# Half of the next block's scores between transposes and values' products in cross attention, and a local gate part behind the fourth transposes

## The chip, the cores and the metric

The kernel runs on one core of one Trainium2 chip. The metric is the device time in microseconds from launch to end of the whole program. A core has TensorE (matmuls and transposes, with weight loads that overlap them), VectorE, ScalarE, GpSimd, and SyncE, which here issues the DMAs. Each engine runs its own list of instructions in order; engines wait for each other on semaphores.

## The reference

One step of a one-layer hybrid decoder for two groups of requests: a prompt of 1024 tokens and 8 samples of 4 tokens each, 1056 tokens in all, with width 1024. All is in 32-bit floats.

```
xn = rmsnorm(x, norm_mix_g)
aq, ak, av, dq, dk, dvv, dz, da, db, ga, gb = split_cols(xn @ w_in)
ya = swa_prompt(aq, ak, av, sinks)          # local attention, window of 128, 8 query heads, 2 key heads
yb = gated_delta(...)                       # 4 heads of 128, chunks
mix = sigmoid(ga) * (ya @ w_br_a) + sigmoid(gb) * (yb @ w_br_b)
h = x + mix @ w_mix_out
hq = (rmsnorm(h, norm_x_g) @ w_xq).reshape(B, L, 4, 128)
s = einsum("blhd,bmhd->bhlm", hq, mem_k) * 128 ** -0.5        # cross attention: 256 memory rows
pr = softmax(s)
xo = einsum("bhlm,bmhd->blhd", pr, mem_v)
h = h + xo @ w_xo
u, gv = split(rmsnorm(h, norm_ffn_g) @ w_up)
h = h + (silu(causal_dwconv(u)) * gv) @ w_down
y = rmsnorm(h, final_norm_g)
```

The change touches the order of TensorE's work in two places: the scores and values of cross attention for the prompt (`s`, `pr`, `xo`), and the product `xn @ w_in` for the gate `ga`, parts of which are done between the steps of local attention (`swa_prompt`).

## The kernel before

Activations stand transposed, width on the partitions and tokens along the free axis. A large product splits each operand into a rounded high part and a remainder (XH and XL, WH and WL) and does three matmuls for each product: high by high, low by high, high by low. GpSimd splits the weights (L746, L748) as they arrive. The stages follow each other: first tiles of `w_in`, local attention, the delta rule, the rest of the gates, branches and mixing, the memory's keys and values, the queries, cross attention, then eleven steps of the MLP.

The order of instructions on each engine is written out by hand; the engines meet through semaphores only.

**Local attention** (`swa_back`, L1373 on) works on eight blocks of 128 queries. For a block c, TensorE does the scores of block c + 1 (L1331), then four groups of four transposes of the probabilities of block c (L1388), each of which waits for VectorE's division (L2091) and for a free bank. ScalarE copies each group from PSUM (L848). After the fourth copy the values' products follow (L1396). Between these steps TensorE does parts of the first gate tiles (`gate_parts`, L1351): a part is three matmuls of 352 columns for one k of eight; eight parts make a unit, and after the last one ScalarE evicts the unit from its one PSUM bank (L826, `gate_out`), for which the first part of the next unit waits (`gate_ev`). How many parts go where is the table in `gates_even` for even c and in `gates_odd` for odd c. In ScalarE's list, the eviction of an even block stands behind its fourth copy; in an odd block there is one ahead of the second half of the exponentials (L842).

**Cross attention** (L1870 on for TensorE, L1191 on for ScalarE, L2483 on for VectorE) works on eight blocks too; blocks 2 to 5 are in a loop. Per block: scores of four heads (L1876, two heads to a bank, two banks b = 0 and 1), two maxima on VectorE, one for each bank (L2486), the scaled negation (L2489), ScalarE's exponentials with sums (L1196), reciprocal (L2500) and division (L2502) on VectorE, eight transposes of 128 x 128 on TensorE (L1887), two copies on ScalarE (L1204), and the values' products (L1893). ScalarE then copies the result rounded (L1188) and VectorE takes the remainder (L2495, `xattn_rest`). VectorE's order for block c:

```
                dve.wait_ge(xa_exp, 4 * c + 4)
                ...
                if not (isinstance(c, int) and c == 0):
                    xattn_rest(c - 1)
                if left:
                    xattn_front(c + 1, 1 - p)       # two maxima, negation
```

ScalarE's order for block c: exponentials of c, rounded copy of c - 1, the queries of c + 2 to their buffer (L1183), the two copies of c. `pipelined` (L552) runs `front(0)` and then `back(c)` for each c.

Of the kernel before, what the change touches and what calls it, by code (L numbers as in the profile page):

```python
# [33 lines left out]
NH = 4  # L34
# [100 lines left out]
def build(nc, d):  # L135
    ctx = ExitStack()
    with ctx:
# [6 lines left out]
        def wait(eng, s, v):  # L144

            if not (isinstance(v, int) and v <= 0):
                eng.wait_ge(s, v)
# [180 lines left out]
        m_kT = dv_flat[:, 0:1024].rearrange("p (h n) -> p h n", h=NH)  # L328
        HQ = TMP[:, 0:4 * T].rearrange("p (h n) -> p h n", h=NH)
        take = carve(4 * T)  # L330
        x_q = take(2 * 512, "p (b h n) -> p b h n", b=2, h=NH)
# [7 lines left out]
        x_ps = lambda h, p: PS[:, X_BANKS[p] + h // 2, NM * (h % 2):NM * (h % 2) + NM]  # L339
# [31 lines left out]
        def end_add(c, m):  # L371
# [5 lines left out]
        hq_ok = sem("hq_ok")  # L377
        xa_st, xa_sc, xa_mx, xa_exp, xa_den, xa_p, xa_tp, xa_pt, xa_pv, xa_hi, xa_lo = [
            sem("xattn_" + x) for x in ("stage", "scores", "max", "exp", "den", "probs", "ptr", "pt", "pv", "hi", "lo")]
# [904 lines left out]
        def _(pe):  # L1284
# [8 lines left out]
            for t in range(6):  # L1293
# [5 lines left out]
                for k in range(KT):  # L1299
# [4 lines left out]
                    mm = gemm_part(t % 2, t % 2, k, KT)  # L1304
# [49 lines left out]
                        mm.then_inc(gate_mm if c < 2 else w_used, 1)  # L1354

            def gates_even(at_, c):
                a, b = {"scores": (0, 3), 0: (3, 4), 1: (4, 6), 2: (6, 8), 3: (8, 8), "values": (8, 12)}[at_]
                gate_parts(c // 2, a, b)

            def gates_odd(at_, c):  # L1360
# [62 lines left out]
            for k in range(NB + 1):  # L1423
                rows = CH if k < NB else TS
                for g in range(2):
                    i = 2 * k + g
                    mm = nc.tensor.transpose(PS[0:rows, i // 4, (i % 4) * CH:(i % 4) * CH + CH],
                                             s_s[:, g, k * CH:k * CH + rows], ident)
# [3 lines left out]
            for g in range(2):  # L1432
                for k in range(NB):
                    nc.tensor.matmul(PS[HD * g:HD * g + HD, 5, 0:CH], s_vc[:, k, HD * g:HD * g + HD], s_pt[:, k, g, :],
                                     start=(k == 0), stop=False)
                mm = nc.tensor.matmul(PS[HD * g:HD * g + HD, 5, 0:CH], s_v[0:TS, HD * g:HD * g + HD],
                                      s_pt[0:TS, NB, g, :], start=False, stop=True)
# [9 lines left out]
            def dn_tile(t, p, norm):  # L1447
# [3 lines left out]
                for k in range(KT):  # L1451
                    mm = gemm_part(p, p, k, KT)
                    if norm and k == KT // 2:
# [4 lines left out]
                        for c in range(2):  # L1458
# [14 lines left out]
                             start=True, stop=True).then_inc(gt_pe, 1)  # L1473
# [247 lines left out]
            for h in range(NH):  # L1721
                mm = nc.tensor.transpose(PS[r, 6, P * h:P * h + P], s_ks[:, h, :], ident)
# [136 lines left out]
            for t in range(4):  # L1859
# [4 lines left out]
                if t == 0:  # L1864
# [2 lines left out]
                gemm_tile(t % 2, t % 2, 0, KT, 0, ready=(nlo, 16) if t == 0 else None,  # L1867
                          between=(lambda: norm_sum(pe, 2), KT - 2) if t == 0 else None).then_inc(w_used, 1)

            def xattn_front(c, p):  # L1870
                pe.wait_ge(xa_st, c + 1)
                if isinstance(c, int) and c == 0:
                    pe.wait_ge(hq_ok, 4)
                wait(pe, xa_exp, 4 * (c - 1))
                for h in range(NH):
                    mm = nc.tensor.matmul(x_ps(h, p), x_q[:, p, h, :], m_kT[:, h, :], start=True, stop=True)  # L1876
                    if h % 2:
                        mm.then_inc(xa_sc, 1)

            def xattn_back(c, p, left):  # L1880
                if left:
                    xattn_front(c + 1, 1 - p)
                pe.wait_ge(xa_p, c + 1)
                wait(pe, xa_pt, 2 * c)
                for i in range(2):
                    for h in range(NH):
                        mm = nc.tensor.transpose(PS[:, 2 + i, CH * h:CH * h + CH], x_s[:, p, h, CH * i:CH * i + CH], ident)  # L1887
                    mm.then_inc(xa_tp, 1)
                pe.wait_ge(xa_pt, 2 * c + 2)
                wait(pe, xa_lo, c)  # L1890
                for h in range(NH):
                    for i in range(2):
                        mm = nc.tensor.matmul(PS[:, 4, CH * h:CH * h + CH], m_v[:, i, P * h:P * h + P], x_pt[:, i, h, :],  # L1893
                                              start=(i == 0), stop=(i == 1))
                mm.then_inc(xa_pv, 1)
# [853 lines left out]
```

## Time and profile before

| | us |
|---|---|
| median of 3 runs | 2023.81 |
| lowest, highest | 2021.89, 2033.92 |
| the profiled execution | 2025.91 |
| its span, first to last instruction | 2024.1 |
| TensorE busy in the span | 1899.2 (94%) |
| VectorE, ScalarE, GpSimd busy | 1001.7, 489.4, 671.2 |
| mean granted TensorE clock | 0.987 |

The profile is of one execution. Its page gives each engine's busy time, the chain of waits that ended last, and groups of instructions by line; the trace behind it can be asked for the order in time, for busy times in a stretch, and for what ended an engine's idle time. In the trace, a matmul of 32-bit floats with 128 x 256 or 128 x 128 columns of data shows as two records, a transpose as one.

### The profile page before, as it was taken

The page shows a single profiled execution, that of the slowest core. Times are in us where ns is not written, and L with a number is a line of the kernel's source. Part 1 is how long each engine was busy: PE and PEld are TensorE (multiplying, and loading weights), DVE is VectorE, ACT ScalarE, POOL GpSimd, SP SyncE. Part 2 cuts the span into 40 slices and gives each one's busy share as a digit, 9 for nine tenths or more (in the row PEclk, how much of TensorE's full clock was granted, in tenths as well). Part 3 has the DMA queues.
Part 4 walks back from the last instruction along what each step waited for, and adds up shares of the span by engine and source line. Part 5 has one row for each costly group of instructions (what it writes and reads, how often), then busy time and mean ns, then how long its engine had stood idle before and what let it go on. Part 6 is the DMA issues. An engine that isn't in the chain of part 4 may idle for free.

```text
span 2024.1 us, 31808 instructions
## 1 busy us (share of the span) xinstructions
PE 1899.2 (94%) x13269; PEld 1786.2 (88%) x13269; DVE 1001.7 (49%) x1150; ACT 489.4 (24%) x908; POOL 671.2 (33%) x333
## 2 busy tenths in 40 slices
PE   6988999999898899999999899999999999999997
PEld 6966899977777788999988699999999999999996
DVE  6767267744554231564142437544454454345356
ACT  6055326632222103412031523100000000000012
POOL 3311033310100122545663024443343343343345
PEclk9999999999999999999999999999999999999998
DMA  4211111110102022422223111111111111111112
GB/s 184 90 38 43 34 43 42 37 59 23 37 26 64 24 68 79 149 85 96 73 84 121 61 39 45 52 42 52 41 41 46 47 41 52 41 41 52 41 46 86
DMA packets 45482, 119.71 MB, mean 59 GB/s; under 512 B 3808, under 2 KB 20896, under 8 KB 44224
## 3 DMA queue, kind: packets, MB, share of 16 engines
q1 hardware_dynamic: 45392, 118.39, 17.8%
q8 instruction: 71, 1.16, 0.2%
q14 instruction: 19, 0.16, 0.0%
HBM read 102.94 MB, written 15.77 MB: 59 GB/s over the span
## 4 chain that ended last, share of the span: by engine, by line
PE 68%; DVE 7%; ACT 3%; issue 2%; DVEq 0%; ACTq 0%
PE PS L533 41%; PE PS L1961 11%; PE PS L1351 3%; PE PS L1549 2%; PE PS L1844 1%; PE PS L1988 1%; PE PS L1587 1%; PE PS L1744 1%; DVE H L2619 1%; ACT TMP L1196 1%; PE PS L1908 1%; PE PS L1929 1%; PE PS L1634 0%; DVE XL L513 0%; PE PS L1901 0%
## 5 line engine op out<-in xcount | busy, mean ns | idle before, releaser
L746 POOL TENSOR_TENSOR WH<-RAW,CST 128x1024 fp32r<-128x1024 f32 x118 | 238.5, 2021 | 1272.3 <-PE PS L533 680.6
L533 PE MATMUL PS<-XH,WH 128*128 128x352 f32 x2280 | 506.3, 330 | 34.0 <-POOL WL L748 13.0
L533 PE MATMUL PS<-XH,WL 128*128 128x352 f32 x2280 | 493.9, 324 | 0.0
L533 PE MATMUL PS<-XL,WH 128*128 128x352 f32 x2280 | 493.6, 325 | 0.0
L533 PEld LDWEIGHTS PS<-XH,WH 128*128 128x128 f32 x2280 | 390.0, 190 | 51.4 <-issue 35.2
L533 PEld LDWEIGHTS PS<-XH,WL 128*128 128x128 f32 x2280 | 393.4, 189 | 0.0
L533 PEld LDWEIGHTS PS<-XL,WH 128*128 128x128 f32 x2280 | 390.2, 189 | 0.0
L748 POOL TENSOR_TENSOR WL<-RAW,WH 128x1024 fp32r<-128x1024 f32 x118 | 317.0, 2686 | 9.3
L2584 DVE TENSOR_TENSOR H<-H,PS 128x1056 f32<-128x1056 f32 x80 | 100.2, 1253 | 130.3 <-PE PS L1961 130.3
L1258 ACT ACTIVATE AH<-TMP 128x1056 fp32r<-128x1056 f32 x20 | 20.8, 1081 | 353.6 <-PE PS L1961 341.1
L1961 PE MATMUL PS<-AH,WH 128*128 128x352 f32 x480 | 103.5, 324 | 1.9 <-DVE H L2584 1.9
L1961 PE MATMUL PS<-AL,WH 128*128 128x352 f32 x480 | 104.1, 325 | 0.0
L1961 PE MATMUL PS<-AH,WL 128*128 128x352 f32 x480 | 103.6, 324 | 0.0
L2597 DVE TENSOR_TENSOR TMP<-TMP,PS 128x1056 f32<-128x1056 f32 x22 | 27.6, 1254 | 151.8 <-PE PS L533 151.8
L1351 PE MATMUL PS<-XH,WH 128*128 128x352 f32 x240 | 87.9, 366 | 7.5 <-ACT DV L826 7.0
L1961 PEld LDWEIGHTS PS<-AH,WH 128*128 128x128 f32 x480 | 81.9, 188 | 2.2 <-DVE H L2584 2.2
L1961 PEld LDWEIGHTS PS<-AL,WH 128*128 128x128 f32 x480 | 81.9, 188 | 0.0
L1961 PEld LDWEIGHTS PS<-AH,WL 128*128 128x128 f32 x480 | 81.7, 188 | 0.0
L1351 PE MATMUL PS<-XH,WL 128*128 128x352 f32 x240 | 77.7, 324 | 0.0
L1351 PE MATMUL PS<-XL,WH 128*128 128x352 f32 x240 | 77.5, 323 | 0.0
L2560 DVE TENSOR_TENSOR TMP<-PS,TMP 128x1056 f32<-128x1056 f32 x22 | 27.6, 1256 | 92.6 <-PE PS L533 92.6
L1351 PEld LDWEIGHTS PS<-XH,WH 128*128 128x128 f32 x240 | 45.4, 189 | 20.9 <-ACT DV L826 10.5
(458 smaller groups left out, 2473.6 us busy)
## 6 DMA issues: line engine op xcount, KB each, us to landing
RAW<-in_w SPq DMA_DIRECT2D x136, 512.0 KB, 3.5
H<-in_xT SPq DMA_DIRECT2D x4, 1056.0 KB, 9.0
TMP<-in_xT SPq DMA_DIRECT2D x2, 2112.0 KB, 8.4
early_gates<-DV SPq DMA_DIRECT2D x18, 176.0 KB, 1.9
out_yT<-H SPq DMA_DIRECT2D x4, 704.0 KB
early_gates<-A SPq DMA_DIRECT2D x12, 176.0 KB, 1.8
DV<-early_gates SPq DMA_DIRECT2D x1, 2112.0 KB, 14.0
TMP<-early_gates SPq DMA_DIRECT2D x2, 1056.0 KB, 5.5
```

The source lines that it names most:

```text
L533: mm = nc.tensor.matmul(PS[:, 3 * mm_g + c, 0:CW], w_[:, p, off + k * P:off + (k + 1) * P], x_[:, xk0 + k, c * CW:(c + 1) * CW], start=fir ...
L746: nc.gpsimd.tensor_tensor(WH[:, p, :], RAW[:, p, :], one, ALU.mult).then_inc(w_hi, 1)
L748: nc.gpsimd.tensor_tensor(WL[:, p, :], RAW[:, p, :], WH[:, p, :].bitcast(F32), ALU.subtract).then_inc(w_split, 1)
L1196: nc.scalar.activation(x_s[:, p, h, :], x_ps(h, p), ACT.Exp, scale=xscale, bias=x_nm[:, p, 1, h:h + 1], accum_out=x_den[:, p, 0, h:h + 1]) ...
L1258: nc.scalar.activation((LASTH if last else AH)[:, i, :], f_act[:, i, :], ACT.Copy).then_inc(f_hi, 1)
L1351: mm = nc.tensor.matmul(PS[:, GATE_BANKS[g >= GA], 0:CW], w_[:, p, k * P:(k + 1) * P], x_[:, k, c * CW:(c + 1) * CW], start=(k == 0 and w_ ...
L1549: mm = nc.tensor.matmul(PS[out, bank + i, HP * j:HP * j + HP], lhs(h, r), rhs(h, r), start=True, stop=True)
L1587: mm = nc.tensor.matmul(PS[:, bank, P * h:P * h + P], lhs(h), rhs(h), start=True, stop=True)
L1961: mm = nc.tensor.matmul(PS[:, 3 * (m % 2) + c, 0:CW], w_[:, p, (m % 4) * 256 + k * P:(m % 4) * 256 + k * P + P], x_[:, k, bass.ts(c, CW)], ...
L2560: nc.vector.tensor_tensor(wide(x[:, 2:2 + T]), acc(i), wide(f_rs), ALU.mult).then_inc(fu_free, 1)
L2584: nc.vector.tensor_tensor(wide(H[:, m, :]), wide(H[:, m, :]), acc(m % 2), ALU.add).then_inc(fd_free, 1)
L2597: nc.vector.tensor_tensor(wide(f_act[:, i, :]), wide(f_act[:, i, :]), acc(i), ALU.mult).then_inc(f_gate, 1)
```

## The change

In cross attention TensorE's scores of block c + 1 are cut in two. Heads 0 and 1 (bank b = 0) stay ahead of the transposes of block c; heads 2 and 3 (bank b = 1) go behind these transposes and ahead of the values' products. In local attention the table for even blocks is changed by one part: part 7, the last one of its unit, goes from behind the third group of transposes to behind the fourth. No instruction is added or taken out, and the order on ScalarE, VectorE, GpSimd and SyncE is as before.

```diff
             def gates_even(at_, c):
-                a, b = {"scores": (0, 3), 0: (3, 4), 1: (4, 6), 2: (6, 8), 3: (8, 8), "values": (8, 12)}[at_]
+                a, b = {"scores": (0, 3), 0: (3, 4), 1: (4, 6), 2: (6, 7), 3: (7, 8), "values": (8, 12)}[at_]
                 gate_parts(c // 2, a, b)
...
+            def xattn_scores(c, p, half):
+                if half == 0:
+                    pe.wait_ge(xa_st, c + 1)
+                    if isinstance(c, int) and c == 0:
+                        pe.wait_ge(hq_ok, 4)
+                    wait(pe, xa_exp, 4 * (c - 1))
+                for h in (2 * half, 2 * half + 1):
+                    mm = nc.tensor.matmul(x_ps(h, p), x_q[:, p, h, :], m_kT[:, h, :], start=True, stop=True)
+                mm.then_inc(xa_sc, 1)
+
             def xattn_front(c, p):
...
+                xattn_scores(c, p, 0)
+                xattn_scores(c, p, 1)
 
             def xattn_back(c, p, left):
                 if left:
-                    xattn_front(c + 1, 1 - p)
+                    xattn_scores(c + 1, 1 - p, 0)
                 pe.wait_ge(xa_p, c + 1)
                 wait(pe, xa_pt, 2 * c)
                 for i in range(2):
                     for h in range(NH):
                         mm = nc.tensor.transpose(PS[:, 2 + i, CH * h:CH * h + CH], x_s[:, p, h, CH * i:CH * i + CH], ident)
                     mm.then_inc(xa_tp, 1)
+                if left:
+                    xattn_scores(c + 1, 1 - p, 1)
                 pe.wait_ge(xa_pt, 2 * c + 2)
```

TensorE's list in the first block of the loop of cross attention, before the change; L1876 are scores of the next block, L1887 transposes, L1893 values' products, and the brackets name the semaphores waited for:

```order
L147 REGISTER_ALU [waits xattn_stage]
L1876 MATMUL PS<-DV,TMP 128x256 [waits xattn_exp]
L1876 MATMUL PS<-DV,TMP 128x256 x3
L1883 REGISTER_ALU
L147 REGISTER_ALU [waits xattn_probs]
L1887 MATMUL PS<-CST,TMP 128x128 [waits xattn_pt]
L1887 MATMUL PS<-CST,TMP 128x128 x7
L1889 REGISTER_ALU
L1893 MATMUL PS<-TMP,DV 128x128 [waits xattn_lo,xattn_pt]
L1893 MATMUL PS<-TMP,DV 128x128 x7
```

The same place in the changed kernel, where L1877 are scores, L1891 transposes and L1899 values' products:

```order
L147 REGISTER_ALU [waits xattn_stage]
L1877 MATMUL PS<-DV,TMP 128x256 [waits xattn_exp]
L1877 MATMUL PS<-DV,TMP 128x256
L1887 REGISTER_ALU
L147 REGISTER_ALU [waits xattn_probs]
L1891 MATMUL PS<-CST,TMP 128x128 [waits xattn_pt]
L1891 MATMUL PS<-CST,TMP 128x128 x7
L1877 MATMUL PS<-DV,TMP 128x256 x2
L1895 REGISTER_ALU
L1899 MATMUL PS<-TMP,DV 128x128 [waits xattn_lo,xattn_pt]
L1899 MATMUL PS<-TMP,DV 128x128 x7
```

Two of the four scores now stand behind the eight transposes, which wait for the division (`xattn_probs`), and ahead of the products' wait for the copies (`xattn_pt`).

TensorE in an even block of local attention, between the third group of transposes and the values' products (L1396), as the difference of the two lists:

```order
 L1351 MATMUL PS<-XL,WH 128x352
 L1351 MATMUL PS<-XH,WL 128x352
-L1351 MATMUL PS<-XH,WH 128x352
-L1351 MATMUL PS<-XL,WH 128x352
-L1351 MATMUL PS<-XH,WL 128x352
 L1388 MATMUL PS<-CST,TMP 128x128 x4
+L1351 MATMUL PS<-XH,WH 128x352
+L1351 MATMUL PS<-XL,WH 128x352
+L1351 MATMUL PS<-XH,WL 128x352
 L1396 MATMUL PS<-TMP 64x512 x4
```

The three matmuls of part 7 went from ahead of the fourth group of transposes to behind it; the fourth group and the values' products are as before.

## Rows read from the trace of the kernel before

**Rows 1.** The page: busy time of TensorE and its share of the span.

```profile
PE 1899.2 (94%) x13269; PEld 1786.2 (88%) x13269; DVE 1001.7 (49%) x1150; ACT 489.4 (24%) x908; POOL 671.2 (33%) x333
```

**Rows 2.** Busy time by engine in two stretches (us, instructions), clock, DMA share, GB/s.

```profile
145.08:172.10 27.02, 23.96 (x152) 18.68 (x152) 19.65 (x36) 14.83 (x49) 4.25 (x2) 1.00 0.12 41
...
1122.90:1145.10 22.20, 19.18 (x130) 16.64 (x131) 13.47 (x24) 16.04 (x49) 0.00 (x0) 1.00 0.00 0
```

**Rows 3.** Chain of waits in cross attention's loop: start, duration in us, what.

```profile
1134.07 1.94 ACT TMP L1196 x8
...
1137.99 1.29 DVE TMP L2486 x2
...
1139.58 1.94 ACT TMP L1196 x8
```

**Rows 4.** Timeline of one block in cross attention: start, duration, engine, line, [idle before].

```profile
1136.24 1.22 DVE L2502 TENSOR_TENSOR TMP<-TMP 128x1024 f32<-128x1024 f32 x1
...
1137.60 1.09 PE L1887 MATMUL PS<-CST,TMP 128*128 128x128 f32 x8
...
1138.29 1.08 ACT L1204 ACTIVATE TMP<-PS 128x512 f32<-128x512 f32 x2 [1.07 <-PE PS L1887]
...
1139.43 2.05 PE L1893 MATMUL PS<-TMP,DV 128*128 128x128 f32 x16 [0.74 <-ACT TMP L1204]
...
1141.31 1.89 PE L1876 MATMUL PS<-DV,TMP 128*128 128x256 f32 x8
...
1143.04 1.08 PE L1887 MATMUL PS<-CST,TMP 128*128 128x128 f32 x8
```

**Rows 5.** Timeline at the head and the end of cross attention.

```profile
1100.15 5.41 PE L1876 MATMUL PS<-DV,TMP 128*128 128x256 f32 x16 [2.07 <-ACT TMP L1183]
...
1103.06 0.69 DVE L2486 TENSOR_REDUCE TMP<-PS 128x2 f32<-128x512 f32 x1 [1.02 <-PE PS L1876]
...
1104.06 0.47 ACT L1196 ACTIVATE TMP<-PS,TMP 128x256 f32<-128x256 f32 x1 [3.44 <-DVE TMP L2489]
...
1107.52 1.60 PE L1887 MATMUL PS<-CST,TMP 128*128 128x128 f32 x8 [1.96 <-DVE TMP L2502]
...
1109.81 3.78 PE L1893 MATMUL PS<-TMP,DV 128*128 128x128 f32 x16 [0.69 <-ACT TMP L1204]
...
1115.80 1.04 PE L1887 MATMUL PS<-CST,TMP 128*128 128x128 f32 x8
...
1148.54 1.09 PE L1887 MATMUL PS<-CST,TMP 128*128 128x128 f32 x8 [1.62 <-DVE TMP L2502]
```

**Rows 6.** TensorE in two stretches of 1 us: busy, granted clock, DMA.

```profile
1108.00:1109.00 1.00, 1.00 (x6) 0.50 0.93 393
...
1147.00:1148.00 1.00, 0.00 (x0) 1.00 0.00 0
```

**Rows 7.** Timeline of an even block of local attention, around the fourth transposes.

```profile
143.31 0.32 PE L1351 MATMUL PS<-XH,WH 128*128 128x352 f32 x1
...
143.79 0.60 PE L1388 MATMUL PS<-CST,TMP 128*128 128x128 f32 x4
...
144.43 0.60 ACT L848 ACTIVATE TMP<-PS 128x512 f32<-128x512 f32 x1 [0.80 <-PE PS L1388]
...
144.92 0.46 ACT L826 ACTIVATE A<-PS 128x352 f32<-128x352 f32 x1
...
145.08 1.94 PE L1396 MATMUL PS<-TMP 128*64 128x512 f32 x8 [0.69 <-ACT TMP L848]
...
146.95 0.43 PE L1351 MATMUL PS<-XH,WH 128*128 128x352 f32 x1
```

**Rows 8.** Timeline of local attention: who starts the next steps.

```profile
153.21 0.46 ACT L826 ACTIVATE A<-PS 128x352 f32<-128x352 f32 x1 [5.78 <-PE PS L1351]
...
155.76 0.16 DVE L2087 TENSOR_TENSOR TMP<-TMP 128x4 f32<-128x4 f32 x1 [5.95 <-ACT H L842]
...
167.30 0.66 PE L1388 MATMUL PS<-CST,TMP 128*128 128x128 f32 x4 [1.41 <-DVE TMP L2091]
```

More of the change, by code:

```diff
@@ L1868, in _ @@
                           between=(lambda: norm_sum(pe, 2), KT - 2) if t == 0 else None).then_inc(w_used, 1)
-            def xattn_front(c, p):
[L1871 to L1878, printed above, removed]
+            def xattn_scores(c, p, half):
[7 more added lines that the diff above has]
+                mm.then_inc(xa_sc, 1)
+            def xattn_front(c, p):
+                xattn_scores(c, p, 0)
+                xattn_scores(c, p, 1)
             def xattn_back(c, p, left):
                 if left:
-                    xattn_front(c + 1, 1 - p)
+                    xattn_scores(c + 1, 1 - p, 0)
                 pe.wait_ge(xa_p, c + 1)
```

## Prediction

> **What bounds the kernel now.** The page's first part has TensorE busy for 94% of the span [rows 1], so almost everywhere a change counts by what it does to TensorE's path. The two stretches that the change touches are the ones where that has to be checked. In local attention a pair of blocks (145.08 to 172.10 us) has TensorE busy for 23.96 of 27.02 us; in the loop of cross attention (1122.9 to 1145.1) for 19.2 of 22.2 us, with ScalarE at 16.0 and VectorE at 13.5 [rows 2]. No engine is full there, so the length of a block is set by a ring of waits.
>
> I read the chain of waits next. In cross attention it goes through no TensorE row between 1122 and 1148 us: exponentials (L1196) at 1134.07, VectorE's reciprocal, division (L2502) and remainder (L2495), the two maxima (L2486, x2) at 1137.99, the exponentials of the next block at 1139.58 [rows 3]. A block is 5.51 us. The timeline shows TensorE beside it: transposes at 1137.60 right behind the division that ends at 1136.24 + 1.22 = 1137.46, ScalarE's copies from 1138.29, 0.74 us idle, values' products at 1139.43, next scores at 1141.31, transposes again at 1143.04 [rows 4]. TensorE's own ring (1137.60 to 1143.04, 5.44 us) is thus nearly as long as the other. What is to be seen: TensorE's scores are done a whole exponential ahead of the maxima that read them. They are off the path because they stand AHEAD of the transposes.
>
> In local attention, an even block has an idle 0.69 us ahead of the values' products at 145.08, because the fourth transposes (143.79) must be copied (144.43) first [rows 7]. Whether that wait is on a ring I read from who starts the next step: ScalarE's gate eviction at 153.21 waited 5.78 us for TensorE's gate part, the division of the odd block then waited for ScalarE (155.76), and TensorE's next even block waited 1.41 us for VectorE at 167.30 [rows 8]. So the ring runs from TensorE (even block, up to the gate parts ahead of the odd transposes) over ScalarE and VectorE back to TensorE: the 0.69 us is on it.
>
> **Local part: the seventh gate part moves behind the fourth transposes.** Three matmuls, from 143.31 to 143.79: 0.48 us of TensorE [rows 7]. In its old place they delay the fourth transposes; these start 0.48 us earlier, ScalarE's copy (the engine is idle for 0.80 us ahead of it, so free from 143.63) starts at 143.95 in place of 144.43, and the products keep their 1.29 us behind the transposes (143.79 to 145.08): they start at 144.60. The moved part now lies in the 0.69 us gap, of which 0.21 is left. Gain: 0.48 us in each of the four even blocks, 4 x 0.48 = 1.9 us. The edit brings a new nearness: the moved part ends unit 0 of the gate, ScalarE must evict it before the part that now follows the products can write the same bank. The eviction starts at 144.92 today, behind the copy; it can keep that order and end by about 144.95, 1.5 us before that part, which comes at 146.95 - 0.48 = 146.47. It costs nothing. ScalarE's next exponentials wait for VectorE, which isn't moved, but they have slack: their division is needed only at the odd block's transposes. Bounds: 0 (if VectorE's ring closes without TensorE) to 1.9 us of gain. I take 1.9, since all four blocks show the same row and the eviction row 153.21 ties the ring to TensorE. No queue of DMAs is passed: nothing but matmuls moves.
>
> **Cross attention: two of the four heads' scores move behind the transposes.** Nothing is added or removed; four blocks' instructions are reordered on TensorE alone. What that frees: the first half runs ahead of the transposes as before, so TensorE can start them some 0.9 us sooner, if their data are there. They are not: the division ends 0.05 to 0.15 us before the transposes start [rows 4]. What it costs: the second maximum (L2486 of bank b = 1) needs scores that can't start until the transposes are through, and those wait for the division. So the ring now takes in TensorE: division, transposes, two scores, second maximum, negation, exponentials, reciprocal, division.
>
> Step by step, from the start T of the transposes. Eight transposes take 1.09 us with their tail [rows 4]; the next matmuls overlap the tail, so I put the half scores' start at T + 0.8. Four heads' scores take 1.89 us from start to end and about 1.73 to the start of the next step (1141.31 to 1143.04) [rows 4]: half of the pace is 0.87, and with the tail of some 0.16 the data are there at T + 1.83. The second maximum starts at T + 1.9. A lone maximum to the exponentials took 1.00 us (1103.06 to 1104.06) [rows 5]. Exponentials to the division's end: 1134.07 to 1137.46, 3.39 us [rows 3, 4]. To the transposes 0.05. The block is then 1.9 + 1.00 + 3.39 + 0.05 = 6.34 us. The first maximum and the remainder of the block before (L2495) fill VectorE only to T + 1.03 (1138.63 today), so they are hidden; ScalarE's copies end at T + 1.77 and the products can start at T + 1.83 as today, so TensorE's 0.74 us of waiting is indeed filled. That gain is worth nothing, since TensorE then waits some 1.7 us for the division.
>
> How many blocks: transposes of block 1 at 1115.80, of block 7 at 1148.54 [rows 5]: 32.74 us for six blocks, 5.46 each. With 6.34 each, 38.0 us: +5.3. Block 0 to 1 is different. There TensorE ran at half clock (0.50 granted at 1108 to 1109) [rows 6], the products of block 0 took 3.78 us and the scores of block 2 held the transposes back until 1115.80 [rows 5]. With the half scores of block 1 behind the transposes of block 0 (1107.52 + 1.4, at half clock 1.7 + 0.3 us) the second maximum comes at 1110.9, the division ends at 1115.3; on TensorE the products end at 1114.2 and the first half of block 2 at 1115.3. Transposes at 1115.4: 0.4 us earlier than now. Together +4.9 us. Ends for the unknown part: the half scores' start between T + 0.75 and T + 1.09 gives a block of 6.3 to 6.6 us, that is +4.6 to +6.5.
>
> The Trainium skill ("TensorE: Matmul & The Clock Gate", step-by-step section of Part 2) says that TensorE may pull weight loads forward but keeps matmuls in program order. The trace agrees so far as the weight loads of the transposes never bring a transpose ahead of the scores; by the rule the late half stays late, and were it not so, this stage would give back about 0.4 us instead of costing 4.9.
>
> **Sum.** -1.9 + 4.9 = +3.0 us. The profiled execution took 2025.91 us with a span of 2024.1, so 1.8 us lie around it; its sum would be 2028.9. The median of the runs shown is 2.1 us lower, 2023.81, and I predict for that: 2026.8, rounded to 2027. What follows both stages (the weights' loads, their splits on GpSimd) waits for TensorE, so either shift passes to the end. A measurement of this kernel can tell about 1%, 20 us, from no change; the three runs alone span 12 us.
>
> **Rivals.**
>
> A, slower: the clock. In the loop TensorE now idles about 1.7 us of each 6.34 us block in one piece, where it idled 0.74 of 5.5. Ahead of block 0's transposes it idled 1.96 us and the clock was at 0.50 right after; before block 7's it idled 1.62 us and stayed at 1.00 [rows 5, 6]. If it falls to the lower level (1.2 GHz) in the loop, transposes take 1.60 in place of 1.09 us and the half scores twice 0.87: +1.4 us a block on the ring, +8.3 for six, and the last products 3.78 in place of 2.05 us, +1.7. Sum +13, 2037. It decides if the clock answers to the new piece as it did to that from 1105.6 to 1107.5. Against it: local attention idles 1.41 us and keeps 1.00. The Trainium skill (same page, section on oscillation) says that idle gaps between bursts throttle the clock again and again, each burst starting cold; half the blocks cold would give 2032.
>
> B, almost even: the two half-clock stretches at the head of cross attention fall elsewhere, since everything comes 1.9 us earlier and other work stands there. Then block 0's transposes come at 1106.6 and block 1's at 1112.9, 2.9 us before today's: 5.3 - 2.9 - 1.9 = +0.5, 2024.
>
> C, faster: the second half is not on a path, because the maximum that waits for it is hidden; the stage is bounded by TensorE's own 5.44 us ring, which the filled 0.74 us shortens until the other ring (5.5) holds. Then -0.4 - 1.9 = -2.3, 2021.5. For it speaks only the block at the loop's start, where TensorE was last; against it the program's order.
>
> D, the local part gives nothing, as VectorE or the eviction closes the ring: +4.9, 2028.7.
>
> **How the numbers follow.** Forecast 0.55 (2024.5 to 2030), A 0.12, B 0.13, C 0.08, D 0.12. From 2021.5 (C) to 2034 (A for half the blocks, and the runs' own spread) leaves out less than 2 in 10. None of these reaches 20 us: faster by over 1% 0.01, slower 0.02 (A with something on top), within 0.97.
>
> **What would show it.** In the profile after: transposes to transposes in the loop 6.3 us (5.5 means C); the second maximum no longer adjacent to the first, idle ahead of it and released by the scores; idle ahead of the transposes about 1.7 us, released by the division; no idle ahead of the values' products; the chain of waits now with TensorE rows in the loop. In local attention the idle 0.69 us becomes 0.2, and a pair of blocks goes from 27.02 to 26.5 us. I am wrong if the clock's row in the loop is below 1.00, or if the block is under 6 us.

## The result, and the profile after

The changed kernel has a median of 2040.64 us (2033.03 to 2042.90, seven executions). The kernel before, in the same session, had 2031.09 (2021.89 to 2033.92, seven). The ratio is 1.0058, with a 95% interval of 1.0034 to 1.0081: 11.8 us slower, between 6.9 and 16.4. That is within 1%, but four times the +3.0 I forecast, and 2040.64 lies above my range. Part of the distance to my 2027 is the base: the kernel before, at 2023.81 in the three executions that I built on, has 2031.09 in these seven. But +11.8 is also more than the range allowed above its own base (2034 - 2023.81 = 10.2).

The profiled execution of the changed kernel took 2033.03 us, and it is the quickest of the seven: its mean granted clock is 0.986, that of the other six 0.980 to 0.982. So two things have to be explained: why this execution is 7.1 us longer than the profiled one of before, and why most are longer still. The page's first part and the line of the chain by engine (compare [rows 1] for the first):

```profile
PE 1900.3 (94%) x13269; PEld 1784.9 (88%) x13269; DVE 1003.6 (49%) x1150; ACT 489.6 (24%) x908; POOL 671.8 (33%) x333
...
PE 68%; DVE 6%; ACT 3%; issue 2%; DVEq 0%; ACTq 0%
```

Busy times are the same to 2 us: nothing was added, so the 7.1 us are waiting. The timeline of one block in cross attention, to be held against [rows 4]; in this kernel L1877 are scores, L1891 transposes, L1899 values' products, L2492 maxima, L2501 the remainder, L2508 the division:

```profile
1131.15 1.23 DVE L2508 TENSOR_TENSOR TMP<-TMP 128x1024 f32<-128x1024 f32 x1
...
1132.51 1.09 PE L1891 MATMUL PS<-CST,TMP 128*128 128x128 f32 x8 [1.93 <-DVE TMP L2508]
1132.89 0.68 DVE L2492 TENSOR_REDUCE TMP<-PS 128x2 f32<-128x512 f32 x1
...
1133.43 1.03 PE L1877 MATMUL PS<-DV,TMP 128*128 128x256 f32 x4
...
1134.34 2.05 PE L1899 MATMUL PS<-TMP,DV 128*128 128x128 f32 x16
1134.50 0.69 DVE L2492 TENSOR_REDUCE TMP<-PS 128x2 f32<-128x512 f32 x1 [0.93 <-PE PS L1877]
...
1139.03 1.09 PE L1891 MATMUL PS<-CST,TMP 128*128 128x128 f32 x8 [1.78 <-DVE TMP L2508]
```

The two maxima stand apart now, the second one after 0.93 us of idleness that TensorE's late scores (L1877) end. The products follow their scores without a wait, and TensorE idles 1.78 us for the division. The chain of waits over the same block:

```profile
1131.15 1.24 DVE TMP L2508
...
1132.51 1.09 PE PS L1891 x8
1133.60 0.88 PE PS L1877 x4
...
1134.50 0.70 DVE TMP L2492
...
1135.51 0.97 ACT TMP L1196 x4
...
1137.68 1.24 DVE TMP L2508
```

Where [rows 3] went through VectorE and ScalarE alone, there are two TensorE rows in each turn. From the transposes at 1112.64 to those at 1151.93 are six blocks and 39.29 us, 6.55 each, where they took 5.46 [rows 5]. The end of the stage. Before, the clock was 1.00 at 1147 to 1148 [rows 6], and the trace has it at 1.00 from 1148 to 1162 too. After:

```profile
1151.93 1.58 PE L1891 MATMUL PS<-CST,TMP 128*128 128x128 f32 x8 [2.57 <-DVE TMP L2508]
...
1154.20 3.78 PE L1899 MATMUL PS<-TMP,DV 128*128 128x128 f32 x16 [0.69 <-ACT TMP L1204]
...
1159.39 1.06 PE L1907 MATMUL PS<-YA,TMP 128*32 128x512 f32 x1 [1.41 <-DVE XL L2501]
```

And busy times by stretch (length, then PE, weight loads, VectorE, ScalarE and GpSimd, the granted clock, the DMA share and GB/s):

```profile
1112.60:1145.50 32.90, 23.75 (x161) 19.88 (x161) 17.37 (x31) 19.58 (x59) 0.00 (x0) 1.00 0.02 7
1156.00:1158.00 2.00, 1.98 (x10) 1.69 (x8) 0.00 (x0) 0.00 (x0) 0.00 (x0) 0.50 0.00 0
1160.00:1162.00 2.00, 2.00 (x4) 0.40 (x3) 0.00 (x0) 0.00 (x0) 0.00 (x0) 0.50 0.00 0
```

In the loop the clock is at its upper level (2.4 GHz, 1.00), but from about 1152 to 1163 us it is at the lower one (1.2 GHz, 0.50), behind the last and longest wait of 2.57 us. The last products take 3.78 us instead of 2.05, and the last of the samples' scores starts 17.3 us after the eighth transposes instead of 13.6: +3.7 us. Local attention does what was forecast. One even block, with the part (L1351) behind the fourth transposes (L1388):

```profile
115.06 0.60 PE L1388 MATMUL PS<-CST,TMP 128*128 128x128 f32 x4
...
115.41 0.41 PE L1351 MATMUL PS<-XH,WH 128*128 128x352 f32 x1
...
116.19 0.46 ACT L826 ACTIVATE A<-PS 128x352 f32<-128x352 f32 x1
...
116.34 1.94 PE L1396 MATMUL PS<-TMP 128*64 128x512 f32 x8 [0.20 <-ACT TMP L848]
```

The idle 0.69 us [rows 7] is 0.20, and the eviction (L826) is out of the way. From the products of this block to those of the next even one are 26.6 us (116.34 to 142.91), 27.0 before [rows 2].

The account of this execution's 7.1 us: the first transposes of cross attention come 3.0 us earlier (1104.52 against 1107.52), 1.9 of it from the four even blocks and the rest because a half-clock stretch at 108 to 112 us of before isn't there. The eight transposes span 47.4 us instead of 41.0: +6.4. The half clock at the end: +3.7. What this execution doesn't hold is the further 7 us or so of the six others; where they are likely to lie, e1, e2 and e3 show below.

### The profile page after: what moved, and what is told of

Same layout as the page of the kernel before. It is cut to its first block, busy times and chain, and to the rows that moved or that the text cites. A ratio compares the mean times of both kernels' runs of the same rounds, so it can differ in the third digit from the quotient of the medians.

```text
span 2031.2 us, 31808 instructions
## 1 busy us (share of the span) xinstructions
PE 1900.3 (94%) x13269; PEld 1784.9 (88%) x13269; DVE 1003.6 (49%) x1150; ACT 489.6 (24%) x908; POOL 671.8 (33%) x333
## 4 chain that ended last, share of the span: by engine, by line
PE 68%; DVE 6%; ACT 3%; issue 2%; DVEq 0%; ACTq 0%
PE PS L533 41%; PE PS L1967 11%; PE PS L1351 3%; PE PS L1549 2%; PE PS L1587 1%; PE PS L1844 1%; PE PS L1994 1%; PE PS L1744 1%; ACT TMP L1196 1%; DVE H L2625 1%; PE PS L1914 1%; PE PS L1935 1%; PE PS L1907 1%; PE PS L1891 0%; PE PS L1877 0%
## 5 line engine op out<-in xcount | busy, mean ns | idle before, releaser
L748 POOL TENSOR_TENSOR WL<-RAW,WH 128x1024 fp32r<-128x1024 f32 x118 | 317.9, 2694 | 9.3
L1351 PE MATMUL PS<-XH,WH 128*128 128x352 f32 x240 | 88.2, 368 | 7.5 <-ACT DV L826 7.0
L1351 PE MATMUL PS<-XH,WL 128*128 128x352 f32 x240 | 77.6, 323 | 0.0
L1351 PE MATMUL PS<-XL,WH 128*128 128x352 f32 x240 | 77.4, 323 | 0.0
L1351 PEld LDWEIGHTS PS<-XH,WH 128*128 128x128 f32 x240 | 45.4, 189 | 20.8 <-ACT DV L826 10.5
```

Source lines behind the costliest of these rows:

```text
L748: nc.gpsimd.tensor_tensor(WL[:, p, :], RAW[:, p, :], WH[:, p, :].bitcast(F32), ALU.subtract).then_inc(w_split, 1)
L1351: mm = nc.tensor.matmul(PS[:, GATE_BANKS[g >= GA], 0:CW], w_[:, p, k * P:(k + 1) * P], x_[:, k, c * CW:(c + 1) * CW], start=(k == 0 and w_ ...
```

## Experiments

Each kernel is compared with the kernel before on the same chip in the same session; e9 to e12 ran on another chip than e1 to e8. A difference "by the medians" is that of two medians; the ratio with its interval is the better measure, and where the two disagree the kernel before's own spread is why: its executions fall into a group of 2021 to 2025 us and one above 2026. The medians of before were 2026.55 us for the first four kernels (26 executions), 2027.87 for the next four (35) and 2027.63 for the last four (27). Beside times I count how many executions have a mean granted clock of 0.985 or less; of before, 38 of 88 have.

**e1: the half scores alone.** The table of local attention as before:

```diff
-                a, b = {"scores": (0, 3), 0: (3, 4), 1: (4, 6), 2: (6, 7), 3: (7, 8), "values": (8, 12)}[at_]
+                a, b = {"scores": (0, 3), 0: (3, 4), 1: (4, 6), 2: (6, 8), 3: (8, 8), "values": (8, 12)}[at_]
```

> Only the cross attention part: two heads' scores behind the transposes, the local table as before. Theory R (the ring of waits takes in TensorE): transposes to transposes 6.5 to 6.7 us in cross attention against 5.5, so +6.4 us from block 0 to block 7, whatever the clock. Theory K (the clock pays besides): the longer idle pieces ahead of the transposes let the granted clock fall to half in part of the executions, at the end of the stage or in it, and the timed runs are 10 to 15 us above before with a mean clock of 0.980 to 0.983. If K is wrong the timed runs are 6 to 8 us above before. Theory L (the local part is what costs): this kernel is level with before.

2033.96 us (2031.31 to 2043.98, 12), ratio 1.0043 [1.0025, 1.0061]: +7.4 by the medians. The profile has the same 47.4 us over the eight transposes and the same half clock from 1150 to 1161; from the first transposes to the last of the samples' scores 64.8 us, 54.6 before: +10.2. In its profile the delta rule, between local attention and the gates, took 240.4 us, 241.9 in that of before. Four of 12 executions are at a clock of 0.985 or less. By my expectation +7.4 would have meant that the clock costs nothing. But the median of before lies between its two groups, and eight of e1's 12 executions are in its own lower one: 2031.31 is the lowest of e1 and 2021.19 that of before, 10.1 us apart, as the stage in the profiles says. (The length of the delta rule here is from the first to the last start of its L1549 matmuls; lengths of the stage of cross attention go from the first transposes to the start of the last of the samples' scores.)

**e2: the local part alone** (the reverse edit of the table, on the kernel before).

> Only the local part: the seventh gate part behind the fourth transposes, cross attention as before. R and K: 1.9 us less than before up to the end of local attention, 0.46 in each of the four even blocks (idle ahead of the values' products 0.2 in place of 0.69 us), and that stays to the end unless half-clock stretches fall otherwise: timed 0 to 4 us below before. L: 5 us or more above before.

2029.86 us (2021.78 to 2032.71, 12), ratio 1.0011 [0.9995, 1.0028]. Not 1.9 faster but, if anything, slower, and between my two expectations (up to 4 us faster; 5 us or more slower). Its profile has the local gain (98.3 us from the first to the last products of the stage, 99.6 before; three of the four even blocks' gains lie between) and loses it several times over in the delta rule. Windows of e2, the whole delta rule and two stretches of it:

```profile
422.60:670.50 247.90, 221.69 (x3055) 188.45 (x3056) 114.97 (x209) 64.76 (x137) 26.25 (x12) 0.96 0.12 37
508.00:512.00 4.00, 4.00 (x33) 3.48 (x33) 1.93 (x4) 1.09 (x3) 0.00 (x0) 0.58 0.46 132
512.00:516.00 4.00, 4.00 (x28) 3.55 (x28) 1.97 (x5) 0.22 (x1) 0.00 (x0) 0.56 0.00 0
```

The same of before:

```profile
426.10:668.50 242.40, 214.40 (x3055) 181.97 (x3056) 114.59 (x209) 64.70 (x137) 26.18 (x12) 0.99 0.12 38
508.00:514.00 6.00, 3.97 (x42) 3.38 (x41) 4.63 (x8) 1.10 (x3) 2.38 (x1) 1.00 0.28 90
```

The same 3055 matmul records take 5.5 us longer. In e2 the clock falls to the lower level in four stretches of the delta rule (466 to 472, 508 to 516, 596 to 602, 638 to 646) and in one right behind it, in before in one (428 to 432). Eleven of 12 executions are at 0.985 or less. What TensorE does ahead of such a stretch, in e2 (first fence) and in before, where no fall follows (second fence; L748 is GpSimd's split of a weight, L2267 an operation of VectorE, shown beside the split and again without it):

```profile
507.83 0.50 PE L1575 MATMUL PS<-TMP 64*64 64x64 f32 x5 [2.02 <-DVE TMP L2342]
```

```profile
467.56 2.70 POOL L748 TENSOR_TENSOR WL<-RAW,WH 128x1024 fp32r<-128x1024 f32 x1
...
468.07 2.75 DVE L2267 TENSOR_TENSOR TMP<-TMP 128x512 f32<-128x512 f32 x1
...
471.20 0.46 PE L1549 MATMUL PS<-TMP,A 64*64 64x64 f32 x16 [1.96 <-DVE TMP L2342]
...
511.32 0.50 PE L1575 MATMUL PS<-TMP 64*64 64x64 f32 x5 [2.03 <-DVE TMP L2342]
...
532.25 0.69 DVE L2267 TENSOR_TENSOR TMP<-TMP 128x512 f32<-128x512 f32 x1
```

The idle pieces of about 2 us are the same in both kernels. Ahead of the one at 471.20 an operation of VectorE takes 2.75 us while GpSimd splits a weight, 0.69 without, and TensorE waits for what follows it. Ahead of the one at 511.32 (507.83 in e2) it is two others, of 1.79 and 1.54 us beside GpSimd's splits, 0.68 elsewhere. No run takes the splits away, so that they slow VectorE is read from this coincidence. Only the pieces' place in time differs, by some 3.5 us, and the clock answers in e2 and not in before.

**e3: the changed kernel with TensorE's wait in cross attention filled** by three useless matmuls in an unread bank, ahead of the wait for the division:

```diff
                     xattn_scores(c + 1, 1 - p, 0)
+                for h in range(3):
+                    nc.tensor.matmul(PS[:, 7, 0:NM], ident, m_kT[:, h, :], start=True, stop=True)
                 pe.wait_ge(xa_p, c + 1)
```

> The changed kernel with three matmuls of 128 x 256 into a bank that nobody reads (bank 7) ahead of each wait for the division, some 1.3 us of useless work where TensorE idles 1.8 us. The ring of waits stays, only TensorE's idleness goes. K: no half clock from block 2 on and at the stage's end; the timed runs are at before + 3 us (ring +6.4, local -1.9, less at the head), mean clock 0.987 or more. If the clock isn't what costs, the timed runs stay where the changed kernel is, at before + 10 to 12 us. Fillers that are late could add up to 0.3 us a block.

2035.98 us (2031.07 to 2038.90, 9), ratio 1.0042 [1.0026, 1.0057]. The blocks stay at 6.5 to 6.7 us, though the wait is a quarter of what it was, and the half clock at the end of the stage is gone:

```profile
1143.91 1.09 PE L1893 MATMUL PS<-CST,TMP 128*128 128x128 f32 x8 [0.49 <-DVE TMP L2510]
...
1150.36 1.09 PE L1893 MATMUL PS<-CST,TMP 128*128 128x128 f32 x8 [0.42 <-DVE TMP L2510]
```

```profile
1156.00:1162.00 6.00, 3.15 (x24) 2.72 (x24) 2.00 (x3) 1.68 (x3) 0.00 (x0) 1.00 0.00 0
```

From the first transposes to the last of the samples' scores it is 59.4 us against 64.7. Of these 5.3 us, 3.7 are the end of the stage and 1.6 the step from block 0 to block 1 (6.46 us for 8.12), which in after had a half-clock stretch too. So the clock's share in this stage is settled, and so is that the ring, not TensorE's load, sets the block. As a whole e3 missed its expectation (+3 us at a mean clock of 0.987 or more): the delta rule is at 248.7 us here, and 8 of 9 executions are at 0.985 or less.

**e4: all four heads' scores behind the transposes** (table of local attention as before):

```diff
                 if left:
-                    xattn_scores(c + 1, 1 - p, 1)
+                    xattn_front(c + 1, 1 - p)
```

> The dose doubled: all four heads' scores behind the transposes, the local table as before. R: the ring takes in two more scores, 0.9 us more a block than with half behind: transposes to transposes 7.4 to 7.6 us at full clock, +12 to +13 us against before over six blocks. K: TensorE idles some 3 us in one piece in each block, the clock falls in most blocks, transposes and scores then take up to twice as long (+2.5 us a block): 25 to 30 us above before. If the clock weren't reached by idleness, 13 to 15 us above before.

2043.46 us (2038.51 to 2048.80, 4), ratio 1.0088 [1.0057, 1.0120]. At full clock a block is 7.3 to 7.5 us, and TensorE idles 2.7 to 2.9 in it:

```profile
1128.28 1.09 PE L1889 MATMUL PS<-CST,TMP 128*128 128x128 f32 x8 [2.79 <-DVE TMP L2506]
...
1135.82 1.09 PE L1889 MATMUL PS<-CST,TMP 128*128 128x128 f32 x8 [2.94 <-DVE TMP L2506]
```

Three other blocks take 8.8 to 9.1 us, around half-clock stretches. Here the clock falls inside the loop, as my rival A had it for the change itself, but not in most blocks, and the 25 to 30 us that I expected of such a clock were 17.

**e5 and e6: is it the local part, or its shift?** Three useless matmuls in each odd block of local attention, ahead of its first gate parts, give back what the part gained. e5 is e2 with them, e6 the kernel before with them:

```diff
+                if c % 2:
+                    for w_, x_ in ((WH, XH), (WH, XL), (WL, XH)):
+                        nc.tensor.matmul(PS[:, 4, 0:CW], w_[:, (c // 2) % 2, 0:P], x_[:, 0, 0:CW], start=True, stop=True)
                 gates("scores", c)
```

> The local part alone, with its gain given back: in each of the four odd blocks three matmuls of 352 columns into a bank that the next transposes overwrite, 0.48 us of useless work ahead of the gate parts. The delta rule then starts as late as before. Theory P (what counts is where in time the delta rule's idle pieces fall against the clock's own rhythm): executions with half clock in the delta rule (mean clock 0.985 or less) are as rare as with the kernel before, about half, and the median is within 2 us of before. Theory S (the change in local attention itself, not its timing, makes them frequent): 8 or more of 10 executions at 0.985 or less, median 4 us or more above before. If the frequent half clock with the local part was chance, half as well.

> The kernel before with the same useless 0.48 us in each of the four odd blocks of local attention: everything behind comes 1.9 us later. All theories: +1.9 us at equal clock. P: the share of executions with a mean clock of 0.985 or less differs from the half that before shows, up or down, since the delta rule is shifted the other way. S: it is about half, as before.

e5: 2022.35 us (2021.06 to 2034.68, 12), ratio 0.9992 [0.9969, 1.0015], 3 of 12 executions at 0.985 or less; I had expected about half, which 12 executions can't tell from 3. e6: 2032.53 (2022.92 to 2036.64, 12), ratio 1.0034 [1.0016, 1.0053], 11 of 12. The delta rule in e5, then in e6:

```profile
423.60:664.50 240.90, 212.93 (x3055) 180.68 (x3056) 114.70 (x209) 64.69 (x137) 26.18 (x12) 1.00 0.12 39
```

```profile
425.00:674.20 249.20, 223.05 (x3055) 189.18 (x3056) 114.89 (x209) 64.77 (x137) 26.17 (x12) 0.95 0.12 37
```

With the gain taken away the extra time of e2 goes too, and a kernel that is only late by 1.9 us has it. So it isn't the local edit as such but its shift in time. That isn't to say that one start of the delta rule is good and another bad: of the profiles, those that start at 421.0 (e3), 422.6 (e2), 422.9 (e12) and 425.0 (e6) have the falls, those at 423.0 (after), 423.5 (e1), 423.6 (e5) and 426.1 (before) don't. Nor do the profiles' starts show the shift of 1.9 us as such: e6, delayed by it, starts 1.1 us earlier than before, which has half-clock stretches at 108 to 112 and 234 to 238 us that e6 hasn't. The shift moves the odds.

**e7 and e8: the delta rule's idle pieces filled.** Six useless matmuls at five places of the delta rule, in e2 (e7) and in the kernel before (e8):

```diff
+            def idle_work(n):
+                for _ in range(n):
+                    nc.tensor.matmul(PS[:, 7, 256:384], ident, ones, start=True, stop=True)
...
+                    if (c, l) in ((1, 4), (2, 6), (3, 7), (5, 4), (6, 6)):
+                        idle_work(6)
```

> The local part alone, with six matmuls of 128 x 128 (1.3 us) into unread columns of bank 7 in five places of the delta rule where TensorE idles 2.0 to 2.6 us for VectorE (behind the gate parts at the borders of the gate's weight tiles). If half clock in the delta rule is what spoils the local gain: no half clock between 430 and 670 us, delta rule 240 to 242 us long, mean clock 0.986 and up in most executions, timed 2 to 6 us below before. If fillers are late: some 0.2 us in each place. If the clock falls all the same, the executions stay at 0.983 and level with before or above.

> The kernel before with the same fillers in the delta rule. If the two groups of times of the kernel before (2021 to 2024 and 2028 to 2034 us) come from half clock in the delta rule, the upper group goes: all executions within 2021 to 2026 us, median 2 to 5 us below before. If they come from elsewhere, both groups stay.

e7: 2022.84 us (2020.06 to 2025.71, 12), ratio 0.9978 [0.9959, 0.9996]. e8: 2021.82 (2021.06 to 2026.76, 12), ratio 0.9979 [0.9964, 0.9995]. None of the 24 executions is at 0.985 or less. In e8 the wait at 471.20 of before is now 0.63 us behind the filling:

```profile
467.16 1.50 PE L1540 MATMUL PS<-CST 128*128 128x128 f32 x12
469.29 0.46 PE L1553 MATMUL PS<-TMP,A 64*64 64x64 f32 x16 [0.63 <-DVE TMP L2348]
```

That shows the idle pieces as what the clock answered to. It doesn't bring the local gain back in the end: e7's profile is 1.5 us shorter than e8's (2020.9, 2022.4), but its median isn't. Its mean clocks are 0.986 to 0.989 against 0.988 to 0.990, so short falls elsewhere may take it; that is argued, not shown.

**e9 and e10: the changed kernel with the delta rule filled** (e9), and with e3's filling as well (e10).

> The changed kernel with the five fillers in the delta rule that left no half clock there in 24 of 24 executions. What is left is ring, local part and the clock at the end of cross attention, by the stage lengths read so far: +10.1 (block 0's transposes to the end of the samples' scores, 64.7 us against 54.6) and -1.9 for the local part, both against the kernel before with the same fillers (2021.8 median): 2030.0. If the half clock of 11 us at the end of cross attention is chance and not caused by the longer idle pieces, part of the executions are at 2026.

> The changed kernel with the fillers in the delta rule and three matmuls of 128 x 256 ahead of each wait for the division in cross attention, so that neither stage has long idle pieces. Left are the ring of waits and the local part: block 0's transposes to the samples' scores' end 59.4 us against 54.6, +4.8 - 1.9 = +2.9 against the kernel before with the delta fillers: 2024.7, which is what the prediction's sum gave (+3.0). If the ring alone cost what the change costs, this kernel would be as slow as the changed one with delta fillers.

e9: 2034.12 us (2029.82 to 2036.99, 10), ratio 1.0039 [1.0024, 1.0055]. e10: 2028.14 (2025.92 to 2031.85, 12), ratio 1.0006 [0.9993, 1.0018]. Filling the delta rule alone leaves the changed kernel 4 us above what I expected (2030.0). The profile, at 2029.82 us the quickest of the ten, doesn't hold these 4 us, but it shows where such time can come from: now the clock falls inside the loop of cross attention.

```profile
1124.23 1.09 PE L1897 MATMUL PS<-CST,TMP 128*128 128x128 f32 x8 [0.81 <-DVE TMP L2514]
...
1130.90 1.09 PE L1897 MATMUL PS<-CST,TMP 128*128 128x128 f32 x8 [1.93 <-DVE TMP L2514]
1131.82 1.66 PE L1883 MATMUL PS<-DV,TMP 128*128 128x256 f32 x4
1133.27 3.01 PE L1905 MATMUL PS<-TMP,DV 128*128 128x128 f32 x16
```

```profile
1118.00:1122.00 4.00, 4.00 (x20) 3.71 (x19) 1.09 (x3) 2.24 (x8) 0.00 (x0) 0.57 0.00 0
1132.00:1136.00 4.00, 4.00 (x19) 3.71 (x19) 0.86 (x2) 2.15 (x9) 0.00 (x0) 0.57 0.00 0
```

Such a block is 7.07 and 7.15 us, the one between them 6.67. In e10 no stretch of the stage is below 1.00, and it is 59.3 us long. Its blocks are as long as those of the changed kernel:

```profile
1110.27 1.09 PE L1899 MATMUL PS<-CST,TMP 128*128 128x128 f32 x8 [0.41 <-DVE TMP L2516]
...
1149.56 1.09 PE L1899 MATMUL PS<-CST,TMP 128*128 128x128 f32 x8 [1.27 <-DVE TMP L2516]
```

That is 39.29 us for six blocks, the same 6.55 each, with TensorE's waits filled and the clock at its upper level. What the ring costs with the clock out of it is read against e11, below.

**e11: the best of both.** The scores as before, the local part, the delta rule filled, and useless matmuls at two more waits: four ahead of the first block's wait for its division, eight ahead of the output product's first wait behind the samples' scores.

```diff
+                if isinstance(c, int) and c == 0:
+                    idle_work(4)
                 pe.wait_ge(xa_p, c + 1)
...
+            idle_work(8)
             pe.wait_ge(xs_dv, 1)
```

> The version that should beat both kernels: local part alone, fillers in the delta rule, four matmuls of 128 x 128 ahead of block 0's transposes in cross attention and eight ahead of the wait for the samples' scores' softmax. Expected 2018 to 2021 us: local -1.9, no half clock in the delta rule, one half-clock stretch less at the head of cross attention (-2.9) or none less if it begins at the block before. Rival: the fillers run at half clock, last twice as long and delay the transposes; then it is level with the version with delta fillers alone, 2022 to 2023.

2020.25 us (2017.15 to 2023.34, 12), ratio 0.9971 [0.9957, 0.9984]: 5.9 us faster than before, and the best of all kernels here. The head of cross attention:

```profile
1103.91 1.05 PE L1540 MATMUL PS<-CST 128*128 128x128 f32 x8
1105.60 1.09 PE L1895 MATMUL PS<-CST,TMP 128*128 128x128 f32 x8 [0.64 <-DVE TMP L2511]
...
1111.05 1.04 PE L1895 MATMUL PS<-CST,TMP 128*128 128x128 f32 x8
```

From block 0's to block 1's transposes it is 5.45 us, 8.28 before [rows 5], and all eight span 38.45 instead of 41.0. The half clock that before has at 1166 to 1170, behind the wait for the samples' softmax, is gone as well. One of the 12 executions shows a mean clock of 0.94 at 2023.34 us, so the mean clock doesn't rank every execution by its time.

e11 and e10 are the two orders of the scores, both with the clock at 1.00 throughout the stage: 52.0 us and 59.3. So the ring costs 7.3 us when no clock is mixed in, and the medians, of the same chip and session, differ by 7.9. The kernel before has 54.6 because its own head is at half clock, the changed one 64.7 because its head and its end are; the difference of 10.1 is 7.3 of ring and 2.8 of clock.

**e12: one head behind the transposes**, three ahead (table of local attention as before):

```diff
-                for h in (2 * half, 2 * half + 1):
+                for h in ((0, 1, 2), (3,))[half]:
```

> Half the dose: three heads' scores ahead of the transposes and one behind, the local table as before. By the ring, the second maximum's data come 0.43 us sooner than with two heads behind: transposes to transposes 6.1 us in the loop (5.5 with none, 6.6 with two, 7.4 with four). If the cost were a fixed one of the split, it would be 6.6.

A single execution, 2038.03 us, with the delta rule at 247.4. The blocks are 6.0 to 6.25 us:

```profile
1132.56 1.09 PE L1892 MATMUL PS<-CST,TMP 128*128 128x128 f32 x8 [0.91 <-DVE TMP L2509]
...
1138.80 1.09 PE L1892 MATMUL PS<-CST,TMP 128*128 128x128 f32 x8 [1.06 <-DVE TMP L2509]
```

With e1 and e4 this is a series: 5.46, 6.1, 6.55 and 7.4 us a block for none, one, two and four heads behind the transposes. The first head costs 0.66 us, because it also puts TensorE's transposes on the ring; each further one costs 0.43, what the scores of one head take (1.73 for four [rows 4]).

## Why the prediction was wrong

**The ring: right in mechanism, a little small in size.** The steps against [rows 4] and my sum: transposes to the second maximum 1.99 us (1132.51 to 1134.50; I had 1.9), maximum to exponentials 1.01 (1.00), exponentials to the division's end 3.39 (1135.51 to 1137.68 + 1.22; 3.39), to the next transposes 0.13 (0.05). That is 6.52 where I had 6.34; the mean of six is 6.55. I put the half scores' start at T + 0.8; it is T + 0.92. The head gave 0.16 us back and not 0.4. The reordering holds for seven turns (blocks 0 to 6), not for the four that one sentence of mine names; the sum had them right. The term "+4.9" measured +6.4, within its ends of 4.6 and 6.5. e3 (TensorE's idleness filled, same block), e4 and e12 (the series) show the ring, e10 against e11 its full price of 7.3 us; rival C is out.

**The local part: the 1.9 us are real where they arise and don't reach the end.** TensorE's waits for the fourth copy sum to 0.8 us in the four even blocks, 2.7 before: the 1.9 of my sum. The first step that failed is the sentence "so either shift passes to the end". I had checked that what follows waits for TensorE, and took it that everything behind then runs as it did, only earlier. It doesn't. In before the delta rule has idle pieces of 2.0 us (the rows of before under e2), and whether the clock falls behind them depends, in its odds, on a shift of 1.9 us: with the local part and nothing to offset it, 25 of 28 executions (e2, e3, after) are at 0.985 or less, before 38 of 88, e1 without it 4 of 12, the gain given back 3 of 12 (e5), a like delay put on before 11 of 12 (e6), the pieces filled 0 of 24 (e7, e8). (In after the count takes in the falls of cross attention as well.) In profiles with the falls the delta rule is 247 to 249 us instead of 240 to 242, and e2's median is 7.5 us above e5's. The term "-1.9" was thus about +2 to +3: e2 is +2.2 by its ratio and +3.3 by its median, and the result's ratio is 3 us above e1's, in two sessions. Rival D had 0. What the falls cost is 7.0 us between the delta rules of e2 (247.4) and e5 (240.4), and 9.3 between their spans.

**The clock in cross attention: rival A, at a place I hadn't named.** This is the second step that failed: the sum has no term for the clock, and A had a chance of 0.12. I asked whether it would fall in the loop. In the changed kernel it fell behind the loop's end and cost 3.7 us (in e3 and e10, with the waits filled, it is gone); in e9, the same stage with another start, also inside the loop. My sign that I'd be wrong, "the clock's row in the loop is below 1.00", looked only at the loop. I read a yes or no from [rows 6], a wait of 1.96 us with a fall and one of 1.62 without, and treated it as a property of the length. Two waits of 1.93 us in after's loop are borne, two of 1.93 in e9's aren't, one of 2.94 in e4's is, and those of 2.0 in the delta rule were borne in one profile and not in the other. The Trainium skill ("TensorE: Matmul & The Clock Gate", section "HAM oscillation") has idle gaps between bursts as what throttles the clock again and again. e9's loop agrees in kind: a cold block alternates with a warm one (7.07, 6.67, 7.15, 6.45 us). But its gaps are 1.93 us, shorter than those of the page's example.

**The sum.** Ring +6.4, its clock +3.7, the local part +2 to +3: some +12.5, against +11.8 measured; e1 (+7.4) and e2 (+3.3) by their medians add to +10.7. I had +3.0. The range failed because I treated rival A and the local gain as separate cases, while both went wrong by the clock's answer to idle pieces.

**Open.** Why a shift of 2 us changes the odds that the clock falls in the delta rule; the trace shows when it falls, not why. Why the medians of e9 and e10 came out 4.1 and 3.4 us above expectation, which nothing in their profiles' cross attention shows. And where the local part's 1.9 us go in e7.

## What to carry to other kernels

Where an engine stands off the ring because its work is done early, its order is part of the ring's length: each piece moved behind the ring's wait adds about its own duration per turn (and the first one also what it waits behind), and the idleness it fills was free. A gain of 2 us in 2000 isn't safe until one knows what its shift does to the clock downstream: look for idle pieces of TensorE of about 2 us anywhere behind the edit (the falls here followed pieces of 1.9 us and more), and compare the mean granted clock over many executions, not in one profile. Where such pieces exist, a few useless matmuls into columns nobody reads gave more than either edit of this change: e8, the kernel before with nothing else, is 4.2 us faster by its ratio, e11 with the local part and two more places 5.9.

## What the runs showed of the hardware

TensorE's clock fell to 0.50 behind idle pieces as short as 1.9 us (e9), not every time (one of 2.94 us in e4 was borne), and stayed there for some 4 to 11 us (1118 to 1122 in e9, 1152 to 1163 in after). A shift of all that follows by 1.9 us changed the share of executions with the falls from 3 in 12 to 11 in 12 (e5, e2). A VectorE operation of 128 x 512 (L2267) took 2.75 us beside GpSimd's split of a weight (2.70 us) and 0.69 us without it; ahead of the delta rule's idle pieces of 2 us stands such an operation, or two others of 1.79 and 1.54 us beside the splits.
